# A fifth slot per weight chunk gets half of its remainder by an accumulating transfer, and the first chunk's table load and gate sums are moved forward

## The chip, the cores and the metric

The kernel runs on one core of a Trainium2 chip. The metric is the device time of one execution in microseconds. The core has five engines that run their own instruction streams and meet through semaphores: TensorE (PE in the profile; PEld is its weight load), VectorE (DVE), ScalarE (ACT), GpSimd (POOL) and SyncE (SP). Transfers are issued by SP (all weights), by POOL and, a few, by ACT.

## The reference, cut to what matters

One decoder block on a sequence of 256 rows of width 2048, in float32:

```python
x = x + 0.5 * swiglu(rmsnorm(x, ffn1_norm), ffn1_wg, ffn1_wu, ffn1_wd)
x = x + hybrid_mixer(rmsnorm(x, mix_norm), ...)      # conv group and sparse attention group
x = x + 0.5 * swiglu(rmsnorm(x, ffn2_norm), ffn2_wg, ffn2_wu, ffn2_wd)
return rmsnorm(x, final_norm)

def swiglu(h, wg, wu, wd):                           # D_FF = 5632
    return (jax.nn.silu(h @ wg) * (h @ wu)) @ wd
```

The change touches the two SwiGLU layers only, called FFN 1 and FFN 2 here (`f` is 0 and 1 in the code).

## The kernel before

**Products in pieces.** Every float32 operand is split into a rounded part and a remainder, `hi` and `lo`. A product is three matmuls: `x_hi w_hi`, `x_hi w_lo` and `x_lo w_hi`. The weights `wg` and `wu` (2048 x 5632) are taken in 11 chunks of 512 columns. A chunk has 16 slots; a slot (a "group") is 256 rows of one of the two matrices, 128 partitions x 2 x 512, and a slot of the kind GATE or UP costs TensorE 12 matmuls of 512 columns: two halves `kk` of the slot, two row tiles of 128, three products. Four slot buffers (`SLOTS = 4`) hold `raw`, `w_hi` and `w_lo`, used in turn. Two neighbouring slots of the kinds PAIR and PAIR2 are computed with seven products in place of eight; for them VectorE makes sums `wt` of the raw weights, and ScalarE and VectorE split these into `wt_hi` and `wt_lo`.

**One slot's way.** SP loads `raw` (512 KB) once `w_lo` of the slot four before is made (`load`). ScalarE rounds it (`hi`, L1365) once the load has landed and TensorE is through with the slot four before. VectorE subtracts (`lo`, L1883) to get `w_lo`. TensorE waits for `lo_ready` in `group` and runs the 12 matmuls (L818 to L820). Each of these engines takes the slots strictly in order, with the other work of a chunk at fixed slots in between.

**Moved slots.** In chunks 2 to 10 (`THREE`), slots 0 to 3 (`MOVED_AT`) have the second half of their remainder made another way. `minus` on ScalarE writes the negated rounded weights into `w_lo[:, s, 1, :]` (L1356), and `remainder` on GpSimd issues a transfer of the weights' 256 KB from HBM that is added to what stands there (L735). VectorE's `lo` then makes only the first half. `group` on TensorE has a branch for these slots (L798, L800, L806): the eight matmuls with `w_hi` first, then the two with the first half of `w_lo`, then a wait for `lo_moved`, then the last two. In the code:

```python
for kk in range(GK):
    if kk:
        pe.wait_ge(lo_moved[s], 16 * moves(c))
    for t, bank in enumerate(banks):
        ins = mm(ps[:, bank, :], hi[:, k + kk, t * P:t * P + P], w_lo[:, s, kk, :], start=False, ...)
```

`minus(c)` is called at the head of `hi(c)`; it waits for the slot's load and for TensorE's end of the slot four before. GpSimd's order in a chunk is: the transfers of moved slots 0 to 3, then the 16 small block transfers of the previous chunk's `gu` (`gu_blocks`, L726), then transfers of moved slots from 4 on, of which there are none before.

**From one chunk to the next.** A chunk's gate products stand in PSUM banks 0 and 1. At its end ScalarE copies product 1 of the pairs (`product1_copy`, L1443); VectorE adds it and the others into the two banks (`gate_products`: L2020, L2005, L2007, L2022; then `right_sums`: L2013, L2015); ScalarE applies Silu to each bank (`silu`, L1459), and TensorE can start the next chunk, which writes the same banks, once both Silus are done (`silu_done`). For the chunks in `LATE` (0 and 2 to 10) this falls into the next chunk: on VectorE `gate_products` comes behind slot 0's `lo`, on ScalarE the copy and the first Silu come behind slot 0's `hi`, and the second Silu behind slot 1's `hi`. ScalarE's functions live in tables. Ahead of chunk 0's Silu the Sqrt table is loaded in both FFNs, so the first Silu of each FFN is preceded by an ACT_TABLE_LOAD.

Of the kernel before, what the change touches and what calls it, by code (L numbers as in the profile page):

```python
# [8 lines left out]
ACT = mybir.ActivationFunctionType  # L9
# [44 lines left out]
          (PAIR, 2), (PAIR2, 2), (UP, 4), (UP, 5), (PAIR, 3), (PAIR2, 3), (UP, 6), (UP, 7)]  # L54
THREE = (2, 3, 4, 5, 6, 7, 8, 9, 10)
LATE = (0,) + THREE
MOVED_AT = (0, 1, 2, 3)
H_QUAD = {1: 0, 2: 1, 3: 2}
PAIRS = 2

# [1 line left out]
def chunk_table(n):  # L62

    return FIRST if n == 0 else CHUNK3 if n in THREE else CHUNK


def chunk_pairs(n):

    return [p for p, (kind, _) in enumerate(chunk_table(n)) if kind == PAIR]
# [22 lines left out]
def chunk_slot(n):  # L92

    return CHUNK_SLOTS * n + (len(down_job(0)) if n >= PART0[1] else 0)
# [65 lines left out]
def moved_slots():  # L160

    return [FFN0[f] + chunk_slot(n) + p for f in range(2) for n in THREE for p in MOVED_AT]

# [140 lines left out]
def build_program(nc, a, out):  # L304
# [45 lines left out]
    junk = sb("junk", [P, CH], BF16)  # L350
# [114 lines left out]
    ones = consts[:, C_ONE:C_ONE + 1]  # L465
# [9 lines left out]
    with ctx:  # L475
# [219 lines left out]
        def _(pool):  # L695
# [42 lines left out]
            def ffn(f):  # L738
                for n in range(1, NFC):
                    early = [p for p in MOVED_AT if p < 4] if n in THREE else []  # L740
                    late = [p for p in MOVED_AT if p >= 4] if n in THREE else []
                    for p in early:
# [587 lines left out]
        def _(act):  # L1330
# [105 lines left out]
            def product1_copy(f, key, last, i=None):  # L1436


                job = job_no(f, key)
                act.wait_ge(pair_done, count(pair_no(f, last) + 1, i, PAIRS))  # L1440
                if job:
                    act.wait_ge(prod_used, count(job, i, 1))
                act.activation(z[:, 0, :], ps[:, PROD1, :], ACT.Copy).then_inc(prod1_copied, 1)  # L1443
# [18 lines left out]
            def late_silu(f, n, t):  # L1462

                if t == 0:
                    product1_copy(f, n, FFN0[f] + chunk_slot(n) + chunk_pairs(n)[-1])
                    if n + 1 not in (PART0[1], NFC):
                        minus(FFN0[f] + chunk_slot(n + 1) + 1)
                silu(f, n, tiles=(t,))
# [397 lines left out]
        def _(dve):  # L1866
# [91 lines left out]
            def slot(f, c, kind, i=None):  # L1958

                if kind == PAIR2:  # L1960
                    s = c % SLOTS
                    dve.wait_ge(hi_ready, count(c + 1, i, CHUNK_SLOTS))
                    tt(w_lo[:, s, 1, :], raw[:, s, 1, :], w_hi[:, s, 1, :].bitcast(F32),
                       ALU.subtract).then_inc(lo_ready, 1)
                    wt_low(f, c - 1, 1, i)
                else:
                    lo(c, i, CHUNK_SLOTS)
                    if kind == PAIR:
                        weight_sums(f, c, i)
                        wt_low(f, c, 0, i)  # L1970
# [46 lines left out]
            def gate_products(f, n, i=None):  # L2017

                dve.wait_ge(prod1_copied, count(job_no(f, n) + 1, i, 1))
                tt(ps[:, 0, :], ps[:, 0, :], z[:, 0, :], ALU.add).then_inc(gate_added, 1)  # L2020
                product_sums(f, n, i)
                tt(ps[:, 1, :], ps[:, 1, :], z[:, 1, :], ALU.add).then_inc(gate_added, 1)  # L2022
# [128 lines left out]
            def ffn(f):  # L2151
                c = FFN0[f]
                if f == 0:
                    first_operands()
                    x_operand(0, 0, 1)
                    op = [lambda n=n: x_operand(0, n) for n in range(NDC)]
                    after = {2: [op[1]], 3: [lambda: h_sums(0, 0, 0)], 4: [op[2]], 5: [lambda: h_sums(0, 0, 1)],
                             6: [lambda: hs_low(0, 0)], 7: [op[3]], 14: [lambda: variance(RS_FFN1, DM, NDC)],
                             15: [lambda: inverse_root(RS_FFN1)]}
                else:  # L2160
                    after = {1: [lambda: residual(NDC - 1, FFN0[1], 1, att_scale)],
                             2: [lambda: h_sums(1, 0, 0), lambda: h_sums(1, 0, 1)], 3: [lambda: hs_low(1, 0)],
                             4: [lambda: variance(RS_FFN2, DM, 3 * NDC)],
                             5: [lambda: x_operand(2, NDC - 1)], 7: [lambda: inverse_root(RS_FFN2)]}
                for p, (kind, _) in enumerate(FIRST):
                    if f == 0 and p == 0:
                        continue
                    slot(f, c + p, kind)
                    for g in after.get(p, ()):
                        g()  # L2170

                def chunk(n, i=None):
                    c = FFN0[f] + chunk_slot(n)
                    gu_at = 9 if n in THREE else 12
                    for p, (kind, _) in enumerate(chunk_table(n)):
                        slot(f, c + p, kind, i)
                        if n == PART0[1]:
                            if p in TURN_STEPS:
                                left_residual(f, 0, 1, TURN_STEPS.index(p))
                            if p == 3:  # L2180
                                right_residual(f, 1)
                        else:
                            if n == 1 and p in (7, 8):
                                h_sums(f, 1, p - 7)
                            if n == 1 and p == 9:
                                hs_low(f, 1)
                            if n - 1 in LATE and p == 0:
                                gate_products(f, n - 1)
                            if n - 1 in LATE and p == 1:
                                right_sums(f, n - 1)  # L2190
                            if p == 2:
                                up_products(f, n - 1, i)
                                up(f, n - 1, i)
                            if p == 3:
                                gu_transpose(f, n - 1, i)
                            if p == gu_at:
                                gu_sums(f, n - 1, quad_no(f, n - 1), i)
                            if p == gu_at + 1:
                                gu_operand(f, n - 1, quad_no(f, n - 1), i)
                            if p == (14 if n in THREE else gu_at + 1):  # L2200
                                gs_low(n - 1, quad_no(f, n - 1), i)
                        if p == 14 and n not in LATE:
                            gate_products(f, n, i)
                        if p == 15 and n not in LATE:
                            right_sums(f, n, i)

                def down(part):
                    c = FFN0[f] + down_slot(part)
                    n_last = PART0[part] + PARTN[part] - 1
                    order = down_job(part)  # L2210
                    steps_at = left_steps(part)
                    for g, (h, p, kind, _) in enumerate(order):
                        slot(f, c + g, kind)
                        if n_last in LATE and g == 0:
                            gate_products(f, n_last)
                        if n_last in LATE and g == 1:
                            right_sums(f, n_last)
                        if g == 2:
                            up_products(f, n_last)
                            up(f, n_last)  # L2220
                        if g == 3:
                            gu_transpose(f, n_last)
                        if g == (12 if part == 0 else 10):
                            gu_operand(f, n_last, None)
                        if g in steps_at:
                            for step in steps_at[g]:
                                left_residual(f, part, *step)
                        if part == 0 and g == HALF[0] + 4:
                            right_residual(f, 0)
                        if part == 1:  # L2230
                            if g == HALF[1] + 2:
                                residual(1, FFN0[f] + down_slot(1, 1), 1, half)
                            if f == 0 and g == X0_AT + 4:
                                x_operand(1, 0)
                            if f == 1 and g in (23, 25, 39):
                                final_gains((23, 25, 39).index(g))

                for n in range(1, PARTN[0]):
                    chunk(n)
                down(0)  # L2240
                for n in range(PART0[1], NFC):
                    chunk(n)
                down(1)
# [468 lines left out]
```

## Time and profile before

| | us |
|---|---|
| median of 3 timed runs | 1812.42 (1812.26 to 1814.29) |
| profiled execution | 1810.13 |
| its span (first to last instruction) | 1808.3 |
| TensorE busy | 1796.8 |
| VectorE busy | 1544.5 |
| ScalarE busy | 1066.0 |
| GpSimd busy | 309.3 |

The granted TensorE clock was 0.999 of full speed (2.4 GHz) over the span. Times in the rows of the next section are counted from the start of the span. A row of instructions names line, engine, operation, and what is written and read (`out<-in`); busy time of an engine that others don't wait for costs nothing. A group of matmuls has overlapping durations: a matmul of 512 columns shows as 389 ns, and in an unbroken stretch one starts every 227 ns.

### The profile page before, as it was taken

What the parts mean: (1) busy time and instruction counts of PE and PEld (TensorE: products, weight loads), DVE (VectorE), ACT (ScalarE), POOL (GpSimd) and SP (SyncE); (2) the same over time, 40 slices, a digit from 0 to 9 for tenths busy, and PEclk for the clock granted to TensorE, in tenths of its full rate; (3) what the DMA queues carried; (4) which work ended last, traced back from release to release, by engine and by line L of the source; (5) the groups of instructions that cost most, each with busy time, mean ns of one, the idle gap of its engine ahead of it and who ended that gap; (6) DMA issues with size and microseconds to landing.
All of it is one profiled execution on the core that took longest, in us unless ns stands there. A gap on an engine that the chain in (4) does not pass through costs nothing.

```text
span 1808.3 us, 22130 instructions
## 1 busy us (share of the span) xinstructions
PE 1796.8 (99%) x8116; PEld 1477.5 (82%) x8116; DVE 1544.5 (85%) x1893; ACT 1066.0 (59%) x1418; POOL 309.3 (17%) x514
## 2 busy tenths in 40 slices
PE   9999999999999999999999999999999999999998
PEld 7778888888888888888788888888888888888886
DVE  7989998889999987678567867899999879999987
ACT  6656655455666556556577745566665455666554
POOL 1123221002222100000123300122221001332100
PEclk9999999999999999999999999999999999999999
DMA  7778876678888767766543655678886677888764
GB/s 244 208 225 244 251 235 210 207 217 239 235 234 242 221 196 210 209 210 198 151 132 114 210 175 182 207 229 241 236 243 213 205 222 224 238 241 249 242 205 151
DMA packets 209661, 386.20 MB, mean 214 GB/s; under 512 B 20164, under 2 KB 25008, under 8 KB 209424
## 3 DMA queue, kind: packets, MB, share of 16 engines
q1 hardware_dynamic: 185008, 352.37, 62.4%
q0 software_dynamic: 22016, 30.90, 8.1%
q10 hardware_dynamic: 2528, 1.52, 0.3%
q8 instruction: 64, 1.05, 0.2%
q14 instruction: 45, 0.37, 0.1%
HBM read 368.98 MB, written 4.19 MB: 206 GB/s over the span
## 4 chain that ended last, share of the span: by engine, by line
PE 90%; DVE 6%; DMA 2%; ACT 1%; issue 1%; SPq 0%; ACTq 0%; DVEq 0%
PE ps L818 18%; PE ps L820 18%; PE ps L819 18%; PE ps L836 7%; PE ps L838 7%; PE ps L837 7%; PE ps L806 3%; PE ps L798 3%; PE ps L800 3%; DVE w_lo L1883 2%; PE ps L885 2%; DMA raw<-in_ffn_wg_dram 1%; DVE wt_lo L1955 1%; ACT w_hi L1365 1%; DVE wt L1945 1%
## 5 line engine op out<-in xcount | busy, mean ns | idle before, releaser
L1883 DVE TENSOR_TENSOR w_lo<-raw,w_hi 128x1024 fp32r<-128x1024 f32 (+1 forms) x567 | 647.7, 1160 | 115.6 <-ACT w_hi L1365 112.2
L1365 ACT ACTIVATE w_hi<-raw 128x1024 fp32r<-128x1024 f32 x567 | 590.4, 1054 | 217.5 <-PE ps L820 130.2
L818 PE MATMUL ps<-w_hi,hT_hi 128*128 128x512 f32 x972 | 381.7, 393 | 1.5 <-ACT gu L1459 1.2
L820 PE MATMUL ps<-w_hi,hT_lo 128*128 128x512 f32 x972 | 378.9, 390 | 0.0
L819 PE MATMUL ps<-w_lo,hT_hi 128*128 128x512 f32 x972 | 378.6, 389 | 0.0
L1416 ACT ACTIVATE wt_hi<-wt 128x1024 fp32r<-128x1024 f32 x176 | 185.5, 1054 | 286.5 <-DVE wt L1945 286.5
L726 POOL DMA_DIRECT2D gu_raw<-gu_sq x352 | 188.4, 544 | 363.5 <-DVE gu_sq L2129 353.4
L818 PEld LDWEIGHTS ps<-w_hi,hT_hi 128*128 128x128 f32 x972 | 182.6, 188 | 39.6 <-DVE w_lo L1883 2.2
L1955 DVE TENSOR_TENSOR wt_lo<-wt,wt_hi 128x1024 fp32r<-128x1024 f32 x176 | 214.6, 1219 | 0.0
L820 PEld LDWEIGHTS ps<-w_hi,hT_lo 128*128 128x128 f32 x972 | 182.5, 188 | 38.8
L819 PEld LDWEIGHTS ps<-w_lo,hT_hi 128*128 128x128 f32 x972 | 182.6, 188 | 36.5
L818 PE MATMUL ps<-w_hi,guT_hi 128*128 128x512 f32 x496 | 193.0, 389 | 0.0
L820 PE MATMUL ps<-w_hi,guT_lo 128*128 128x512 f32 x496 | 193.0, 389 | 0.0
L819 PE MATMUL ps<-w_lo,guT_hi 128*128 128x512 f32 x496 | 192.9, 389 | 0.0
L735 POOL DMA_DIRECT2D w_lo<-in_ffn_wg_dram x72 | 62.3, 866 | 648.4 <-ACT w_lo L1356 648.4
L1945 DVE TENSOR_TENSOR wt<-raw 128x1024 f32<-128x1024 f32 x88 | 107.5, 1221 | 23.9 <-PE ps L838 10.6
L798 PE MATMUL ps<-w_hi,hT_hi 128*128 128x512 f32 x288 | 112.1, 389 | 0.0
L800 PE MATMUL ps<-w_hi,hT_lo 128*128 128x512 f32 x288 | 112.1, 389 | 0.0
L819 PEld LDWEIGHTS ps<-w_lo,guT_hi 128*128 128x128 f32 x496 | 93.1, 188 | 19.4
L820 PEld LDWEIGHTS ps<-w_hi,guT_lo 128*128 128x128 f32 x496 | 93.1, 188 | 19.4
L818 PEld LDWEIGHTS ps<-w_hi,guT_hi 128*128 128x128 f32 x496 | 93.1, 188 | 19.2
L765 POOL TENSOR_SCALAR prob<-prob,sums,gate 128x128 f32<-128x128 f32 (+1 forms) x64 | 37.2, 590 | 258.8 <-DVE sums L2391 258.8
(320 smaller groups left out, 2790.1 us busy)
## 6 DMA issues: line engine op xcount, KB each, us to landing
raw<-in_ffn_wu_dram SPq DMA_DIRECT2D x176, 512.0 KB, 5.1
raw<-in_ffn_wd_dram SPq DMA_DIRECT2D x176, 512.0 KB, 4.8
raw<-in_ffn_wg_dram SPq DMA_DIRECT2D x175, 512.0 KB, 4.6
raw<-in_w_in_dram SPq DMA_DIRECT2D x88, 512.0 KB, 3.7
w_lo<-in_ffn_wg_dram POOLq DMA_DIRECT2D x72, 256.0 KB, 6.7
raw<-in_w_out_dram SPq DMA_DIRECT2D x32, 512.0 KB, 4.5
gu_raw<-gu_sq POOLq DMA_DIRECT2D x352, 32.0 KB, 3.6
x_parked<-x SPq DMA_DIRECT2D x8, 256.0 KB, 5.3
```

The source lines that it names most:

```text
L726: pool.dma_start(gu_raw[c_ * SQ:c_ * SQ + SQ, :, a_, :], gu_sq[a_ * SQ:a_ * SQ + SQ, :, c_ * P:c_ * P + P]).then_inc(gu_moved, 16)
L798: mm(ps[:, bank, :], hi[:, k + kk, t * P:t * P + P], w_hi[:, s, kk, :], start=begin, stop=False, skip_group_check=skip)
L800: mm(ps[:, bank, :], lo[:, k + kk, t * P:t * P + P], w_hi[:, s, kk, :], start=False, stop=False, skip_group_check=skip)
L818: mm(o, x_hi, w_hi[:, s, kk, :], start=begin, stop=False, skip_group_check=skip)
L819: mm(o, x_hi, w_lo[:, s, kk, :], start=False, stop=False, skip_group_check=skip)
L820: ins = mm(o, x_lo, w_hi[:, s, kk, :], start=False, stop=last and kk == GK - 1, skip_group_check=skip)
L836: mm(o, x_hi, y_hi, start=start, stop=False, skip_group_check=True)
L837: mm(o, x_hi, y_lo, start=False, stop=False, skip_group_check=True)
L1365: act.activation(w_hi[:, c % SLOTS, :, :], raw[:, c % SLOTS, :, :], ACT.Copy).then_inc(hi_ready, 1)
L1416: act.activation(wt_hi[:, 2 * half:2 * half + 2, :], wt[:, 2 * half:2 * half + 2, :], ACT.Copy).then_inc(t_hi_ready, 1)
L1883: tt(w_lo[:, s, 0:own, :], raw[:, s, 0:own, :], w_hi[:, s, 0:own, :].bitcast(F32), ALU.subtract).then_inc(lo_ready, 1)
L1955: tt(wt_lo[:, sl, :], wt[:, sl, :], wt_hi[:, sl, :].bitcast(F32), ALU.subtract).then_inc(t_lo_ready, 1)
```

## The change

Three edits, which all act in both FFNs:

1. `MOVED_AT` gets slot 14. In chunks 2 to 10 the slot (UP, 6) is then a moved slot too: ScalarE writes the negated half ahead of its `w_hi`, GpSimd issues the accumulating transfer (behind `gu_blocks`), VectorE makes half of `w_lo`, and TensorE runs the other branch of `group`, with its wait.
2. On ScalarE a Silu of one element is put behind `product1_copy` of chunk 0, so that the table load belongs to it and not to the first Silu of `gu`.
3. On VectorE `gate_products` of chunk 0 goes from behind slot 0 of chunk 1 to ahead of it.

```diff
--- before.py
+++ after.py
@@ -54,7 +54,7 @@
           (PAIR, 2), (PAIR2, 2), (UP, 4), (UP, 5), (PAIR, 3), (PAIR2, 3), (UP, 6), (UP, 7)]
 THREE = (2, 3, 4, 5, 6, 7, 8, 9, 10)
 LATE = (0,) + THREE
-MOVED_AT = (0, 1, 2, 3)
+MOVED_AT = (0, 1, 2, 3, 14)
 H_QUAD = {1: 0, 2: 1, 3: 2}
 PAIRS = 2
 
@@ -1463,6 +1463,8 @@
 
                 if t == 0:
                     product1_copy(f, n, FFN0[f] + chunk_slot(n) + chunk_pairs(n)[-1])
+                    if n == 0:
+                        act.activation(junk[:, 0:1], ones, ACT.Silu)
                     if n + 1 not in (PART0[1], NFC):
                         minus(FFN0[f] + chunk_slot(n + 1) + 1)
                 silu(f, n, tiles=(t,))
@@ -2173,6 +2175,8 @@
                     c = FFN0[f] + chunk_slot(n)
                     gu_at = 9 if n in THREE else 12
                     for p, (kind, _) in enumerate(chunk_table(n)):
+                        if n == 1 and p == 0:
+                            gate_products(f, n - 1)
                         slot(f, c + p, kind, i)
                         if n == PART0[1]:
                             if p in TURN_STEPS:
@@ -2184,7 +2188,7 @@
                                 h_sums(f, 1, p - 7)
                             if n == 1 and p == 9:
                                 hs_low(f, 1)
-                            if n - 1 in LATE and p == 0:
+                            if n - 1 in LATE and p == 0 and n > 1:
                                 gate_products(f, n - 1)
                             if n - 1 in LATE and p == 1:
                                 right_sums(f, n - 1)
```

## Rows read from the trace of the kernel before

**Rows 1.** The page, busy us of each engine with share and count

```profile
PE 1796.8 (99%) x8116; PEld 1477.5 (82%) x8116; DVE 1544.5 (85%) x1893; ACT 1066.0 (59%) x1418; POOL 309.3 (17%) x514
```

**Rows 2.** TensorE's waits: waited for, us in total, times, longest

```profile
PE ps L818 <- ACT gu L1459: 1.2, 1, 1.2
PE ps L836 <- DVE wt_lo L1955: 0.7, 2, 0.5
```

**Rows 3.** Timeline, TensorE, chunk 0 to 1 of FFN 1: start us, length us, what

```profile
54.50 0.39 PE L820 MATMUL ps<-w_hi,hT_lo 128*128 128x512 f32 x1
56.06 0.50 PE L818 MATMUL ps<-w_hi,hT_hi 128*128 128x512 f32 x1 [1.18 <-ACT gu L1459]
```

**Rows 4.** Timeline, ScalarE, the same place; in brackets idle time and what ended it

```profile
50.17 0.57 ACT L1443 ACTIVATE z<-ps 128x512 f32<-128x512 f32 x1
52.51 1.28 ACT L1459 ACT_TABLE_LOAD   x1 [1.76 <-DVE ps L2020]
53.80 0.69 ACT L1459 ACTIVATE gu<-ps,rs 128x512 f32<-128x512 f32 x1
54.38 1.05 ACT L1365 ACTIVATE w_hi<-raw 128x1024 fp32r<-128x1024 f32 x1
55.33 0.68 ACT L1459 ACTIVATE gu<-ps,rs 128x512 f32<-128x512 f32 x1
```

**Rows 5.** Timeline, VectorE, the same place

```profile
51.73 0.69 DVE L2020 TENSOR_TENSOR ps<-ps,z 128x512 f32<-128x512 f32 x1
...
53.78 0.70 DVE L2022 TENSOR_TENSOR ps<-ps,z 128x512 f32<-128x512 f32 x1
55.47 1.23 DVE L1883 TENSOR_TENSOR w_lo<-raw,w_hi 128x1024 fp32r<-128x1024 f32 x1 [0.99 <-ACT w_hi L1365]
...
64.00 2.32 DVE L1883 TENSOR_TENSOR w_lo<-raw,w_hi 128x1024 fp32r<-128x1024 f32 x2
```

**Rows 6.** Chain that ended last, first and last of 14 pieces before TensorE

```profile
117.80 1.23 DVE wt L1945
...
124.27 1.15 DVE w_lo L1883
```

**Rows 7.** Groups of instructions, ScalarE: busy us, mean ns, idle us before

```profile
L1411 ACT ACT_TABLE_LOAD x2 | 2.6, 1283 | 0.0
```

**Rows 8.** Groups by shape, VectorE, `w_lo` of whole and of moved slots

```profile
L1883 DVE TENSOR_TENSOR w_lo<-raw,w_hi 128x1024 fp32r<-128x1024 f32 x495 | 599.6, 1228 | 103.0 <-ACT w_hi L1365 100.0
L1883 DVE TENSOR_TENSOR w_lo<-raw,w_hi 128x512 fp32r<-128x512 f32 x72 | 49.3, 687 | 12.6 <-ACT w_hi L1365 12.2
```

**Rows 9.** Timeline, slot 14: `w_hi` and 11th matmul, first and last of 18

```profile
132.42 1.99 ACT L1365 ACTIVATE w_hi<-raw 128x1024 fp32r<-128x1024 f32 x2
138.40 0.39 PE L819 MATMUL ps<-w_lo,hT_hi 128*128 128x512 f32 x1
...
1684.57 1.04 ACT L1365 ACTIVATE w_hi<-raw 128x1024 fp32r<-128x1024 f32 x1
1692.52 0.39 PE L819 MATMUL ps<-w_lo,hT_hi 128*128 128x512 f32 x1
```

**Rows 10.** Timeline, chunk 8 of FFN 1, slot 0: negated copy, transfer's issue

```profile
466.81 0.63 ACT L1356 ACTIVATE w_lo<-raw 128x512 fp32r<-128x512 f32 x1 [0.78 <-DMA raw<-in_ffn_wg_dram]
...
467.74 0.93 POOL L735 DMA_DIRECT2D w_lo<-in_ffn_wg_dram  x1 [17.93 <-ACT w_lo L1356]
```

**Rows 11.** Line L735, its 72 accumulating transfers: who waited (us, times); landing

```profile
PEld ps L806: 0.8, 4
...
DMA to landing us min/median/max: 4.2/6.7/7.8
```

**Rows 12.** Windows around the end of chunk 7, FFN 1; last: clock, DMA share, GB/s

```profile
460.00:465.00 5.00, 5.00 (x24) 4.14 (x23) 4.93 (x7) 3.40 (x5) 0.00 (x0) 1.00 0.50 127
...
470.00:475.00 5.00, 5.00 (x24) 4.14 (x23) 4.62 (x8) 4.46 (x8) 1.68 (x2) 1.00 1.05 320
```

**Rows 13.** DMA issues, one chunk's first accumulating transfer (slowest of 18): KB, landing us

```profile
w_lo<-in_ffn_wg_dram POOLq DMA_DIRECT2D x1, 256.0 KB, 7.2
```

## The prediction

> **What bounds the kernel now.** The page comes first: TensorE is busy for 1796.8 of 1808.3 us [rows 1]. The sum is made against this execution: the program took 1810.13 us, 1.83 us more than its span, and the median of the three timed runs, 1812.42 us, lies 2.29 us above that. I assume both offsets stay, so a change of the span is added to the median.
>
> The second view is what TensorE waited for. It names one wait worth having, 1.2 us for ScalarE's `gu` (the second Silu of a chunk), and 0.7 us for `wt_lo`; the rest is smaller [rows 2]. The reader is to see how little there is to win: TensorE goes from matmul to matmul, one every 0.227 us in a stretch without a wait, and no edit to another engine's work can give more than the few waits listed. A gain beyond 0.2% (3.6 us, about what a measurement of this kernel tells from no change) isn't there to be had; a loss is, because TensorE would wait for anything that comes late, 18 times over.
>
> **Part one: the table load.** TensorE's last matmul of chunk 0 in FFN 1 starts at 54.50 and the next at 56.06 [rows 3]. Undisturbed, that one starts at 54.50 + 0.227 = 54.73, so the stall is 1.33 us. ScalarE's rows show its end: copy of product 1 to 50.74, idle 1.76 us, table load 1.28 us from 52.51, Silu, `w_hi` of chunk 1's slot 1, second Silu to 56.01 [rows 4]. The load waits there because it belongs to the Silu, which waits for VectorE's first add into `ps`; that add starts only at 51.73, after `w_lo` of chunk 1's slot 0 [rows 5].
>
> After the change the load has nothing to wait for: 50.74 to about 52.03, plus about 0.2 us for one element. VectorE turns to the sums when the copy is there, 50.78. From its rows the four adds take 53.78 + 0.70 - 51.73 = 2.75 us, to 53.53. The first Silu runs 52.2 to 52.9, `w_hi` to 53.8, the second Silu to 54.5. The moved `w_lo` comes after the sums, 53.43 to 54.65. TensorE needs both, so it starts at about 54.75 and the stall shrinks by 1.3 us. What is queued behind VectorE's new wait is that `w_lo` and everything after; the load of slot 4's weights on SyncE's queue waits for it too, and leaves near 54.7, some 2.8 us later. What hides that is VectorE's order: slot 4's `w_lo` has its turn only at 64.00 [rows 5], 63.1 in the new order, and with 1.05 us for `w_hi` ahead of it the load would have to take over 7.3 us to be late; if it does, the 0.9 us below shrink by as much.
>
> Of the 1.3 us not all stays. VectorE's next `w_lo` started at 55.47 behind 0.99 us of idle time [rows 5]; in the new order it starts at 54.57, 0.9 us earlier. The chain of waits runs through VectorE alone from 117.80 to 125.42 in chunk 2, and only then passes to TensorE, which it makes wait for `w_lo` [rows 6]. There the two engines meet again, and what is left is what VectorE gained: **0.9 us**. The bounds are 0 (all given back) and 1.4.
>
> In FFN 2 the same place holds no stall: the wait for `gu` is counted once in the whole span [rows 2]. There the moved `w_lo` leaves idle time in front of the sums and goes behind them, where VectorE waited 0.99 us in FFN 1 as well. Gain 0; loss at most 0.2, its 1.2 us less that idle time.
>
> A rule was weighed here. ScalarE's rows show two Sqrt table loads of 1283 ns with 0.0 us of idle time before them [rows 7], so a load follows on what went before. The Trainium skill, "ScalarE: Activation LUTs", section "What ACT_TABLE_LOAD costs", gives the same 1283 ns but adds about 1380 ns of drain to each switch; its load would end near 53.4, the Silus would end near 55.7, and only some 0.3 us would be won. The trace contradicts it, and the sum goes by the rows.
>
> **Part two: the 15th slot.** Nine chunks of each FFN gain one moved slot, 18 in all. For each, VectorE's `w_lo` shrinks from 1228 to 687 ns [rows 8], 18 x 0.54 = 9.7 us of VectorE, none of it on TensorE's clock in most chunks. ScalarE gets a negated copy of 0.63 us [rows 10] ahead of `w_hi`: 18 x 0.63 = 11.3 us on an engine busy for 59% [rows 1]. VectorE's `w_lo` of the slot starts up to 0.6 us later and is 0.54 us shorter, so it is ready when it was. GpSimd gets 18 issues of about 0.93 us [rows 10]; the 16 block transfers of the chunk are through by then. The 18 transfers move 4.7 MB more.
>
> What has to be on the path is the transfer itself. It can't start before the negated copy, and that copy stands on ScalarE where `w_hi` of the slot stands now, behind the pair's two `wt_hi`. TensorE needs the sum at the slot's 11th matmul, 10 x 0.227 = 2.27 us after its first. In chunk 2 of FFN 1 `w_hi` starts at 132.42 and the 11th matmul at 138.40: 5.98 us. In chunk 10 of FFN 2 it is 1684.57 and 1692.52: 7.95 us [rows 9]. Read alike, the 18 budgets are 5.98, 6.51, 7.17, 7.91, 8.46, 6.95, 7.02, 6.46, 7.16 in FFN 1 and 5.99, 6.75, 7.04, 7.91, 8.47, 7.73, 6.07, 6.95, 7.95 in FFN 2.
>
> Against that stands copy, issue and landing. From a copy's start to GpSimd's issue it is 467.74 - 466.81 = 0.93 us [rows 10]. From issue to landing the 72 transfers of this kind took 4.2 to 7.8 us, median 6.7 [rows 11]. Which of these is the new one like? The later three of a chunk stand in each other's way: DMA is 1.05 busy in 470 to 475, and moves 320 GB/s, against 0.50 in 460 to 465 just before the new issue [rows 12]. The first of each chunk (18 of them) took 4.2 to 7.2 us, mean 5.8 [rows 13]. The new one, earlier and alone, is nearest to these.
>
> - At 4.2 us: 5.13 in all, below every budget, cost 0.
> - At 5.8 us: 6.73 in all. Five budgets are short, by 0.75, 0.22, 0.27, 0.74, 0.66: 2.6 us.
> - At the median 6.7 us: 7.63 in all. Twelve are short: 11.5 us.
> - At the longest, 7.8 us, all are short: 28.7 us.
>
> I take **1.2 us**, below the 5.8 line, for two reasons. The stretch ahead of the new issue is the emptiest of a chunk. And VectorE, which paces ScalarE up to this slot, gets 0.54 us back in each chunk, so from the second of these chunks on the negated copy comes earlier; the two chunks 2 have no such help and are the shortest, 0.75 us each at 5.8.
>
> The new transfer also stands before the next chunk's four. TensorE already waits for four of the 72, 0.8 us in all [rows 11]. 256 KB at the 300 GB/s of that stretch is 0.85 us; 4 x 0.85 = 3.4 is the upper bound, 0 the lower (a wait in the 15th slot gives the others time). I take **0.3 us**.
>
> **Sum.** -0.9 + 1.2 + 0.3 = +0.6 us: the span goes to 1808.9, the profiled execution to 1810.7, and the median to **1813.0 us**.
>
> **Rivals.**
> - *The transfer lands late nearly everywhere.* For it: half of the 72 took 6.7 us or more, and the budgets hardly exceed 8. Against it: the empty stretch, and that first ones run at 5.8. It decides from a landing of about 6.1 us, where the shortfalls sum to 4.6 us and, with 0.3 and less 0.9, the result is slower by over 0.2%. At 6.7 it is 11.5 + 0.3 - 0.9: 1823 us; half the shortfall, should VectorE's help count, gives 1817.6. Chance 0.19. The Trainium skill, "SBUF — State Buffer", section "SBUF: two separate sides", warns that VectorE can lock GpSimd out of the port through which it writes a transfer's descriptors, which would push this way; the trace shows one issue of 0.93 us [rows 10] beside a VectorE that is busy for 85% [rows 1], and nothing that tells such a lock from GpSimd's own pace.
> - *No transfer is late.* If it lands in under 5 us, part two costs nothing, the waits for `wt_lo` (0.7 us [rows 2]) may go, and the time is 1812.4 - 0.9 to 1812.4 - 1.8: 1811.1 us. Within 0.2%. Chance 0.25.
> - *VectorE's relief is worth more than the waits show.* Matmuls after a wait start slowly, and the waits of [rows 2] may understate what small lags add up to. TensorE would have to shed 3.6 us; all its idle time is 11.5 us, the start and the end of the program within it [rows 1]. Chance 0.03: 1808.
> - *The forecast*, 1811.8 to 1815: chance 0.53.
>
> **Range and chances.** 1810.8 to 1817.5 us. Below it lies most of the third rival and a little spread of the runs (1812.26 to 1814.29 before), above it half of the first; about 0.2 together. Faster by over 0.2% (below 1808.8): 0.03. Slower (above 1816.0): 0.19. Within: 0.78.
>
> **What would show the steps.** Right: the table load of FFN 1 at about 50.8, right behind the copy; TensorE's gap at 54.5 below 0.2 us; a wait for `w_lo` in chunk 2 no smaller than now. 90 transfers with the new ones at 5 to 6 us; TensorE's waits for `DMA w_lo` at 1 to 2 us in all, in chunks 2 first, and VectorE's busy time down by some 10 us. Wrong: waits for `DMA w_lo` in most chunks, summing to over 4.5 us; or a gap at 54.5 as before, which would mean that the load, or the moved `w_lo`, doesn't run where I put it. What would upset the sum is a landing time off by 0.4 us, since the budgets lie so close to it.

## The result and the profile after

The change makes the kernel slower: a median of 1819.58 us (12 executions, 1814.75 to 1822.27) against 1812.45 us for the kernel before (12 executions in the same session, 1811.34 to 1815.21). The ratio (of the means, here and below) is 1.0035, 95% interval 1.0028 to 1.0043: a small loss, but clear of the noise. The prediction, 1813.0 us in a range of 1810.8 to 1817.5, had the direction, a forecast of 0.6 us more, and missed the size, 7.1 us more, which lies outside its range. Its first rival, "the transfer lands late nearly everywhere", gives the place of the loss; the trace shows it at ten of 18 places.

The page of the kernel after, span and busy time of each engine (compare [rows 1]):

```profile
span 1819.1 us, 22185 instructions
...
PE 1802.8 (99%) x8115; PEld 1477.8 (81%) x8116; DVE 1537.8 (85%) x1893; ACT 1073.0 (59%) x1438; POOL 324.9 (18%) x532
```

ScalarE and GpSimd do more (20 and 18 instructions), VectorE less. TensorE's waits in the kernel after (waited for: us in total, times, longest; compare [rows 2]):

```profile
PE ps L806 <- DMA w_lo<-in_ffn_wu_dram: 4.1, 6, 1.0
...
PE ps L836 <- DVE wt_lo L1957: 0.9, 3, 0.5
PE ps L806 <- DMA w_lo<-in_ffn_wg_dram: 0.8, 2, 0.5
```

Two things stand out. The 1.2 us for `gu` is gone, and a new wait for `w_lo<-in_ffn_wu_dram` has come: slot 14 is of the kind UP, the only moved slot that reads `wu`, so this name is the new transfer and no other. The view lists the larger waits only, and counts each from the end that it gives the matmul before, so each comes out some 0.2 us short. Measured from start to start of the two matmuls around the wait for `lo_moved`, less the 0.227 us of an undisturbed step, slot 14 waits in 10 of 18 chunks, 6.0 us in all, and slots 2 and 3 of the next chunk wait 1.6 us.

The transfers' own rows, in the list of issues of the kernel after (count, KB each, median us from issue to landing):

```profile
w_lo<-in_ffn_wg_dram POOLq DMA_DIRECT2D x72, 256.0 KB, 6.5
...
w_lo<-in_ffn_wu_dram POOLq DMA_DIRECT2D x18, 256.0 KB, 6.0
```

**Slot 14 of chunk 2, step by step.** ScalarE, GpSimd and TensorE in the timeline of the kernel after (compare [rows 9, 10]):

```profile
133.75 0.61 ACT L1356 ACTIVATE w_lo<-raw 128x512 fp32r<-128x512 f32 x1
...
134.66 0.94 POOL L735 DMA_DIRECT2D w_lo<-in_ffn_wu_dram  x1 [18.00 <-ACT w_lo L1356]
...
139.26 0.61 PE L806 MATMUL ps<-w_lo,hT_hi 128*128 128x512 f32 x2
140.53 0.73 PE L806 MATMUL ps<-w_lo,hT_hi 128*128 128x512 f32 x2 [0.65 <-DMA w_lo<-in_ffn_wu_dram]
```

The copy starts at 133.75 and the issue at 134.66, 0.91 us later. The issue sees its data land 5.83 us after that, at 140.49, and TensorE goes on at 140.53. It would have gone on at 139.26 + 2 x 0.227 = 139.71: a budget of 5.96 us (I had read 5.98), where copy, issue and landing took 6.74, and 0.82 us lost.

**The front.** ScalarE at the end of chunk 0 of FFN 1, kernel after (compare [rows 4]):

```profile
52.04 0.58 ACT L1443 ACTIVATE z<-ps 128x512 f32<-128x512 f32 x1
52.63 1.28 ACT L1467 ACT_TABLE_LOAD   x1
53.93 0.21 ACT L1467 ACTIVATE junk<-consts 128x1 bf16<-128x1 f32 x1
54.04 0.68 ACT L1459 ACTIVATE gu<-ps,rs 128x512 f32<-128x512 f32 x1
```

The load stands right behind the copy, and the Silu right behind the one element. TensorE there, kernel after (compare [rows 3]; everything is 1.8 us later here, see below):

```profile
56.35 0.39 PE L820 MATMUL ps<-w_hi,hT_lo 128*128 128x512 f32 x1
56.73 0.47 PE L818 MATMUL ps<-w_hi,hT_hi 128*128 128x512 f32 x1
```

The gap went from 1.33 to 0.38 - 0.23 = 0.15 us.

**Where the 10.8 us of the two spans are.** 1.8 us have nothing to do with the change: they arise before the first product matmul. TensorE's start, kernel before:

```profile
5.01 0.66 PE L912 MATMUL ps<-consts,x 128*128 128x128 f32 x4
...
7.92 0.50 PE L927 MATMUL ps<-w_hi,hT_hi 128*128 128x512 f32 x1
```

and kernel after:

```profile
5.73 1.12 PE L912 MATMUL ps<-consts,x 128*128 128x128 f32 x4
...
9.74 0.50 PE L927 MATMUL ps<-w_hi,hT_hi 128*128 128x512 f32 x1
```

Such starts come and go between profiled executions, without regard to the edit: in this form (product matmul at 9.5 or later) it shows in six profiles of the eleven experiments too, five show the other. So I compare profiles from the end of chunk 0 on. The first matmul of chunk 2, kernel before:

```profile
98.56 0.39 PE L798 MATMUL ps<-w_hi,hT_hi 128*128 128x512 f32 x1
```

and kernel after:

```profile
99.58 0.39 PE L798 MATMUL ps<-w_hi,hT_hi 128*128 128x512 f32 x1
```

It is 1.02 us later, so 0.8 us of the 1.8 have been won back by the front. From there to the end the distance grows to 10.8 us, by 9.8: 6.0 + 1.6 us are the waits measured above. The remaining 2.1 us are mostly their shadow: behind each of these 14 waits the second matmul, too, starts 0.11 us late (0.338 us after the first in place of 0.227), which makes 1.5 us. About 0.6 us is left in gaps that I haven't put down to single waits. The medians differ by 7.1 us; a profile is one execution, and its 10.8 us hold the slow start.

### The profile page after: what moved, and what is told of

The parts are those of the page before. It is cut to its first block, busy times and chain, and to the rows that moved or that the text cites. A ratio compares the mean times of both kernels' runs of the same rounds, so it can differ in the third digit from the quotient of the medians.

```text
span 1819.1 us, 22185 instructions
## 1 busy us (share of the span) xinstructions
PE 1802.8 (99%) x8115; PEld 1477.8 (81%) x8116; DVE 1537.8 (85%) x1893; ACT 1073.0 (59%) x1438; POOL 324.9 (18%) x532
## 4 chain that ended last, share of the span: by engine, by line
PE 69%; DVE 14%; DMA 10%; ACT 3%; issue 3%; POOL 1%; ACTq 0%; DVEq 0%; SPq 0%; POOLq 0%
PE ps L818 15%; PE ps L820 15%; PE ps L819 15%; PE ps L836 5%; PE ps L838 4%; PE ps L837 4%; DVE w_lo L1885 4%; DMA raw<-in_ffn_wg_dram 3%; DMA raw<-in_ffn_wu_dram 3%; DMA w_lo<-in_ffn_wu_dram 2%; PE ps L806 2%; DVE wt L1947 2%; DVE wt_lo L1957 2%; PE ps L798 2%; PE ps L800 2%
## 5 line engine op out<-in xcount | busy, mean ns | idle before, releaser
L1885 DVE TENSOR_TENSOR w_lo<-raw,w_hi 128x1024 fp32r<-128x1024 f32 (+1 forms) x567 | 639.6, 1142 | 129.0 <-ACT w_hi L1365 124.1
L819 PE MATMUL ps<-w_lo,hT_hi 128*128 128x512 f32 x900 | 351.1, 390 | 0.0
L820 PEld LDWEIGHTS ps<-w_hi,hT_lo 128*128 128x128 f32 x900 | 169.0, 188 | 36.1
L818 PEld LDWEIGHTS ps<-w_hi,hT_hi 128*128 128x128 f32 x900 | 169.2, 188 | 35.4 <-DVE w_lo L1885 1.6
L819 PEld LDWEIGHTS ps<-w_lo,hT_hi 128*128 128x128 f32 x900 | 169.1, 188 | 33.7
L735 POOL DMA_DIRECT2D w_lo<-in_ffn_wg_dram x72 | 61.2, 850 | 382.8 <-ACT w_lo L1356 381.9
L806 PE MATMUL ps<-w_lo,hT_hi 128*128 128x512 f32 x360 | 100.4, 394 | 5.4 <-DMA w_lo<-in_ffn_wu_dram 4.1
```

What stands on the lines that cost most here:

```text
L818: mm(o, x_hi, w_hi[:, s, kk, :], start=begin, stop=False, skip_group_check=skip)
L819: mm(o, x_hi, w_lo[:, s, kk, :], start=False, stop=False, skip_group_check=skip)
L820: ins = mm(o, x_lo, w_hi[:, s, kk, :], start=False, stop=last and kk == GK - 1, skip_group_check=skip)
L1885: tt(w_lo[:, s, 0:own, :], raw[:, s, 0:own, :], w_hi[:, s, 0:own, :].bitcast(F32), ALU.subtract).then_inc(lo_ready, 1)
```

## The experiments

Each kernel was timed beside the kernel before; all ratios are to it, with 95% intervals. "Waits" are measured from start to start as above, and landings, where a mean is given, are worked out from the 18 transfers of that slot. Where a diff is against the kernel after, it says so.

**One part alone.** Edits 2 and 3 without slot 14 (e1; against after: `MOVED_AT = (0, 1, 2, 3)`).

> Edits 2 and 3 alone (table load and gate sums of the first chunk moved forward; slots 0 to 3 moved as before). Theory A (the loss is the fifth slot's, the front edits win what was forecast): 0.8 to 0.9 us below the kernel before, about 1811.6 us, TensorE's gap between chunk 0 and 1 of FFN 1 at about 0.15 us. Rival B (the front edits cost something later on, for instance through the later load of chunk 1's slot 4): 1 us or more above the kernel before.

Measured: 1810.90 us, ratio 0.9996 [0.9988, 1.0005]. From the end of chunk 0 to the end of chunk 1 the profile is 0.84 us shorter than before's. Then slot 14 without edits 2 and 3 (e2; diff against before):

```diff
-MOVED_AT = (0, 1, 2, 3)
+MOVED_AT = (0, 1, 2, 3, 14)
```

> Edit 1 alone (slot 14 moved, the front as before). Theory A: 7 us above the kernel before, some 1819.5 us, with waits of TensorE for the 15th slot's transfer of 6 us and of 1 to 2 us for slots 2 and 3. Rival B (the front edits share in the loss): within 4 us of the kernel before.

Measured: 1817.99 us, ratio 1.0034 [1.0022, 1.0046]; 6.6 us of waits in slot 14 at a mean landing of 6.15 us, and 0.1 us in slots 0 to 3. Its waits on TensorE:

```profile
PE ps L806 <- DMA w_lo<-in_ffn_wu_dram: 5.1, 8, 1.3
...
PE ps L818 <- ACT gu L1459: 1.2, 1, 1.2
```

The whole loss is slot 14's; the front, about 0.8 us, lies below what these timings tell from nothing. And this profile, which began as the one of before did (chunk 0 ends within 0.05 us of it), ends 7.9 us later: 6.7 us of waits and 11 times the 0.11 us behind a wait.

**The transfer or its surroundings?** (e3) The kernel after with all that slot 14 got but the transfer: VectorE makes the whole remainder over the negated copy, so the same sum is computed, and TensorE keeps the order of matmuls of a moved slot (diff against after; `KEPT` are the 18 slots).

```diff
-    return sum(1 for m in MOVED if m <= c and m % SLOTS == c % SLOTS)
+    return sum(1 for m in MOVED if m not in KEPT and m <= c and m % SLOTS == c % SLOTS)
...
-                    late = [p for p in MOVED_AT if p >= 4] if n in THREE else []
+                    late = []
...
-                own = 1 if c in MOVED else GK
+                own = 1 if c in MOVED and c not in KEPT else GK
```

> The changed kernel, but slot 14's transfer isn't issued and VectorE makes the whole remainder; ScalarE's negated copy and TensorE's other order of matmuls stay. Theory A (the lateness of the transfer is the cost): the loss is gone, 0 to 1 us below the kernel before, 1811.5 to 1812.5. Rival C (ScalarE's extra 0.63 us ahead of w_hi, or TensorE's other branch, is the cost): still 5 us or more above the kernel before.

Measured: 1811.78 us, ratio 0.9998 [0.9989, 1.0007]. ScalarE's copy and the other order of matmuls cost nothing that can be seen; the transfer and VectorE's shorter share make the 0.37% between this kernel and the one after.

**Another slot.** (e4, against after.)

```diff
-MOVED_AT = (0, 1, 2, 3, 14)
+MOVED_AT = (0, 1, 2, 3, 15)
```

> The changed kernel with slot 15 moved in place of slot 14. In the trace before, w_hi of slot 15 starts at 464.98 in chunk 7 and the 11th matmul of that slot comes at 473.7: a budget of 8.7 us where slot 14 had 6.95. Copy, issue and landing took 6.5 to 8.9 us for slot 14. Theory A (a budget too short by some tenths): waits for this slot's transfer fall from 6.0 to below 1 us and the time to about 1812 to 1813.5, the rest being the next chunk's slots. Rival D (the extra 4.7 MB in a crowded stretch is the cost, whichever slot it belongs to): 1817 us or more.

Measured: 1820.24 us, ratio 1.0051 [1.0035, 1.0068]. Slot 15 itself waits 0.4 us in all, with budgets of 7.7 to 9.5 us and a mean landing of 6.7 us. But the waits have moved, as TensorE's list shows:

```profile
PE ps L806 <- DMA w_lo<-in_ffn_wg_dram: 3.6, 6, 1.1
...
PE ps L806 <- DMA w_lo<-in_ffn_wu_dram: 0.2, 1, 0.2
```

Slots 0 to 3 of the next chunk wait 0.2, 2.7, 0.6 and 1.8 us, and land on average after 7.25 us in slot 0 and 7.03 in slot 1, against 6.44 and 5.91 in the kernel after. The budget is longer by 1 us or more, and the kernel is no faster: the waits are at the next transfers, which this one stands before.

**The same transfer, asked for earlier.** (e5) ScalarE makes the negated half ahead of slot 13's work in place of behind it (against after):

```diff
                     for p, (kind, _) in enumerate(chunk_table(n)):
+                        if p == 13:
+                            minus(c + 14)
                         slot(f, c + p, kind, i)
```

> The changed kernel with slot 14's negated copy made ahead of slot 13's w_hi on ScalarE, some 1.5 us earlier (in the trace before that place is 462.56 in chunk 7, against 464.03). Theory A (slot 14's budgets are some tenths short of 7.1 us for copy, issue and landing): waits for slot 14 fall from 6.0 to below 0.7 us. If the waits are all there is to it, the time is 1811 to 1813. Theory D, added since the run with slot 15 (a transfer also pushes its neighbours in the queue): the earlier one is further from the next chunk's, whose waits stay at 0 to 2 us. Rival C (ScalarE's extra work ahead of the pair's second half is the cost): waits for wt_lo of over 3 us appear instead, and the time stays above 1817.

Measured: 1812.45 us beside 1811.88 before, ratio 1.0004 [0.9995, 1.0014]. ScalarE and GpSimd in chunk 2:

```profile
131.18 0.62 ACT L1356 ACTIVATE w_lo<-raw 128x512 fp32r<-128x512 f32 x1
131.70 0.61 ACT L1424 ACTIVATE w_hi<-raw 128x512 fp32r<-128x512 f32 x1
132.22 1.04 ACT L1416 ACTIVATE wt_hi<-wt 128x1024 fp32r<-128x1024 f32 x1
133.16 2.00 ACT L1365 ACTIVATE w_hi<-raw 128x1024 fp32r<-128x1024 f32 x2
...
132.09 0.94 POOL L735 DMA_DIRECT2D w_lo<-in_ffn_wu_dram  x1 [15.76 <-ACT w_lo L1356]
```

The copy stands ahead of 1.5 us of other ScalarE work (131.70 to 133.16) in place of behind it. The budgets become 7.4 to 9.5 us, 8.7 on average, the 18 transfers land after 5.8 us on average, and slot 14 waits nowhere. It is the same transfer, as large, in the same chunk; only its start is earlier, and the loss of 0.35% is gone.

**The same transfer, asked for later.** (e6) The copy goes behind `w_hi` of the slot, and the load that reuses the buffer waits for it as well (against after):

```diff
+                if c - SLOTS in LATE_COPY:
+                    sp.wait_ge(minus_ready, MOVED.index(c - SLOTS) + 1)
...
-                minus(c)
+                late = c in LATE_COPY
+                if not late:
+                    minus(c)
...
+                if late:
+                    minus(c)
```

> The changed kernel with slot 14's negated copy behind the slot's w_hi instead of ahead of it, about 1 us later; all work is the same (SyncE's load of the slot four further on waits for the copy as well). Theory A: every budget is 0.95 to 1.05 us shorter; with a landing of 6.2 us the shortfalls add up to 17 to 19 us, and the time is near 1829. Theory D alone (what counts is the amount moved, not when it starts): under 1822.

Measured: 1840.53 us, ratio 1.0158 [1.0144, 1.0172]; 22.4 us of waits in slot 14, mean landing 7.09 us. TensorE's list, in which one name now holds nearly all:

```profile
PE ps L809 <- DMA w_lo<-in_ffn_wu_dram: 19.9, 15, 3.3
```

With the early copy this is a scale of three marks for one and the same transfer: ahead of 1.5 us of ScalarE's work, no waits; as changed, 6.0 us; behind `w_hi`, 22.4 us. Why it was more than expected: copy to use, without the stall, measures 6.80 us on average against 7.11, and the landing is 7.09 against 6.21, so of the 1.2 us that each slot is worse off, 0.3 are the lost budget and 0.9 a slower landing, which I had not foreseen. What made it slower isn't shown: the edit also holds back the load that reuses the buffer. The median is 28.7 us above before's, more than the waits; the last section shows what follows on a long one.

**Do the neighbours hold it up?** (e7) Slot 0 is no longer a moved slot, so that a chunk has four transfers as before (against after):

```diff
-MOVED_AT = (0, 1, 2, 3, 14)
+MOVED_AT = (1, 2, 3, 14)
```

> The changed kernel without slot 0 in the list: slots 1, 2, 3 and 14 are moved, so there is as much transferred as before the change and nothing follows slot 14's transfer for about 5 us. Theory A (the landing of slot 14's own transfer is too long for its budget, whoever follows): slot 14's landing stays near 6.1 us and its waits at 4 to 6 us, time 1815 to 1818. Theory D (the neighbours make it slow): its landing falls to 5.3 us or less and its waits below 1.5 us, time 1811 to 1813.

Measured: 1814.60 us beside 1811.88 before, ratio 1.0011 [1.0002, 1.0020]. Slots 1 to 3 no longer wait at all, slot 14 still does:

```profile
PE ps L806 <- DMA w_lo<-in_ffn_wu_dram: 2.8, 5, 0.7
```

Its waits are 4.1 us from start to start at a mean landing of 6.06 us, against 6.21 in the kernel after. So slot 14's landing isn't the work of the transfer that follows it. What a fifth transfer costs the following ones is less certain. They wait nowhere here and 1.6 us in the kernel after; but slots 0 to 3 also wait 0.75 us in e1 and 0.7 us in e3, where there is no fifth transfer, and only 0.1 us in e2, where there is one.

**Half the bytes.** (e9) Slot 14's transfer moves 128 KB, VectorE makes the other columns (against after, the core; `width` is used in the negated copy too):

```diff
+                width = CH // 2 if c in HALVED else CH
+                pool.dma_start(w_lo[:, s, 1, 0:width], w[:, GK * q + 1, n * CH:n * CH + width],
                                accum_op=ALU.add).then_inc(lo_moved[s], 16)
...
+                if c in HALVED:
+                    cols = slice(CH // 2, CH)
+                    tt(w_lo[:, s, 1, cols], raw[:, s, 1, cols], w_hi[:, s, 1, cols].bitcast(F32), ALU.subtract)
```

> The changed kernel with half of slot 14's transfer: 256 of its 512 columns (128 KB) come by the accumulating transfer and ScalarE's negated copy is as much shorter, VectorE makes the other 256. Theory A: copy, issue and landing get shorter by 0.3 us for the copy and by whatever of the landing's 6.2 us goes with its size; with a landing near 5.2 us the waits fall below 0.5 us and the time to 1811 to 1812.5. Rival E (the landing is mostly a fixed time or time spent behind the raw loads issued before it): landing 5.8 us or more, waits above 2 us, time 1814 or more.

Measured: 1813.88 us beside 1812.07 before, ratio 1.0008 [0.9999, 1.0017]. The list of issues has:

```profile
w_lo<-in_ffn_wu_dram POOLq DMA_DIRECT2D x18, 128.0 KB, 5.3
```

Half the bytes land on average after 5.4 us in place of 6.2, only 0.8 us sooner; the shorter copy gives another 0.2 us. Slot 14's waits fall to 0.4 us, slots 1 to 3 keep 1.4 us, about what the time lies above the 1812.5 us that I had expected at most. Most of a landing isn't bytes.

**The front's two edits one by one.** Edit 2 alone (e8, against before: the one-element Silu only), and edit 3 alone (e10, against before: `gate_products` ahead of slot 0 only).

> Edit 2 alone: the one-element Silu that carries the table load, with VectorE's order as before. From the rows of the kernel before the first Silu starts at about 52.5 instead of 53.80, slot 1's w_hi ends at 54.2, the second Silu waits for the second bank's sum (54.48) and ends at 55.2: TensorE's gap is 0.5 to 0.6 us instead of 1.33. If what is won in the end is VectorE's earlier w_lo of slot 1 (55.47, now 54.4), TensorE is 0.8 to 1.0 us ahead at the end of chunk 1, as with both edits. If edit 3 is what wins, 0.3 us or less is left there.

> Edit 3 alone: VectorE's sums of chunk 0 ahead of its w_lo, the table load where it was. From the rows of the kernel before the load waits for the first sum (51.5), ends at 52.8, the Silus at 53.5 and 55.2: TensorE's gap 0.5 to 0.6 us, as with edit 2 alone, and 0.8 to 0.9 us won at the end of chunk 1. If the forecast's reason (VectorE's earlier w_lo of slot 1) is right, edits 2 and 3 are alternatives, not terms of a sum: both together won 0.84, edit 2 alone 0.92.

Measured: edit 2 alone 1810.34 us beside 1811.88 before, ratio 0.9993 [0.9984, 1.0002]; edit 3 alone 1811.13 us beside 1812.07, ratio 0.9997 [0.9988, 1.0006]. The times tell neither from nothing; the profiles do. From the end of chunk 0 to the end of chunk 1, edit 2 saves 0.92 us, edit 3 saves 0.82, and both together 0.84. TensorE's place with edit 2 alone:

```profile
54.55 0.39 PE L820 MATMUL ps<-w_hi,hT_lo 128*128 128x512 f32 x1
55.36 0.50 PE L818 MATMUL ps<-w_hi,hT_hi 128*128 128x512 f32 x1 [0.42 <-ACT gu L1459]
```

The gap is still 0.58 us, more than with both, and yet nothing is lost by the end of chunk 1: there VectorE's lead decides and not the gap, as the prediction had it. The kernel after shows where the difference goes. With both edits TensorE comes 0.42 us (start to start) too early for VectorE's next `wt_lo`:

```profile
85.14 0.50 PE L836 MATMUL ps<-wt_hi,hs_hi 128*128 128x512 f32 x1 [0.26 <-DVE wt_lo L1957]
```

With edit 2 alone there is no wait at this place. The two edits are alternatives.

**What the experiments point to.** (e11) Edit 2 alone, slots 1, 2, 3 and 14, and the early copy (diff against before):

```diff
-MOVED_AT = (0, 1, 2, 3)
+MOVED_AT = (1, 2, 3, 14)
...
                     product1_copy(f, n, FFN0[f] + chunk_slot(n) + chunk_pairs(n)[-1])
+                    if n == 0:
+                        act.activation(junk[:, 0:1], ones, ACT.Silu)
...
+                        if p == 13:
+                            minus(c + 14)
                         slot(f, c + p, kind, i)
```

> A version put together from the runs so far: edit 2 alone at the front, slots 1, 2, 3 and 14 moved (as many as before the change), slot 14's negated copy ahead of slot 13's w_hi. With an early copy slot 14 should have no wait, and with slot 0 out of the list slots 1 to 3 none either (in the run with slots 1, 2, 3 and 14 they had 0.0 us). Theory A: 0.8 to 1.8 us below the kernel before, and no better than edit 2 alone, since TensorE has nothing else to shed: 1810 to 1811. If it is slower than the kernel before, something other than the transfers' lateness comes with slot 14.

Measured: 1809.17 us beside 1812.07 before, ratio 0.9984 [0.9975, 0.9993]: 0.16% faster than the kernel before, with the same number of transfers, and clearly faster than the kernel after. What the moved slots add to edit 2 isn't shown: edit 2 alone had 0.9993 [0.9984, 1.0002], and the intervals overlap. No wait for a transfer is left in any of the 72 places. The largest wait on TensorE outside the start is

```profile
PE ps L818 <- ACT gu L1459: 1.2, 3, 0.4
```

## Why the prediction was wrong

**Right: the front.** Load behind the copy, the gap below 0.2 us (0.15), 0.9 us left of it by chunk 2 where VectorE paces (0.83 in the kernel after, 0.92 with edit 2 alone). What I missed is that either edit alone gives the whole. The load in its new place starts right behind the copy and the next operation right behind the load, so the drain of 1380 ns that the Trainium skill, "ScalarE: Activation LUTs", section "What ACT_TABLE_LOAD costs", adds to a switch isn't to be seen after the change either.

**Right: the mechanism and its arithmetic.** Budgets by slot 14's copy and 11th matmul, less copy, issue and landing, were the right account. The 18 unstalled budgets measured after have a mean of 7.11 us (mine had 7.14), copy to issue 0.91 us (I had 0.93). The prediction named a landing of 6.1 us as the point from which the result is slower by over 0.2%. It is 6.21 us (5.63 to 7.99), and put into my own table of budgets, with 0.91 for copy to issue, this gives 5.5 us; 6.0 us were measured. What the sum had no term for is the 0.11 us behind each wait, 1.5 us in all. e5 and e6 show the same balance from both sides.

**The step that failed** is the value that the prediction took out of this arithmetic: "I take **1.2 us**, below the 5.8 line, for two reasons." Measured: 6.0 us. Both reasons fell.

- *"The stretch ahead of the new issue is the emptiest of a chunk."* True, and beside the point: a transfer lives in the stretch behind its issue. The stretch behind it, which I had not read, in the kernel before, and under it chunk 2's two in the kernel after (columns as in [rows 12]: TensorE, its loads, VectorE, ScalarE, GpSimd, then granted clock, DMA share, GB/s):

```profile
465.00:470.00 5.00, 5.00 (x24) 4.14 (x23) 4.82 (x6) 3.63 (x6) 0.93 (x1) 1.00 0.82 243
```

```profile
130.00:135.00 5.00, 4.97 (x23) 3.79 (x22) 4.93 (x7) 3.69 (x5) 0.34 (x1) 1.00 0.57 144
135.00:140.00 5.00, 4.88 (x22) 3.71 (x20) 4.83 (x7) 3.33 (x5) 1.46 (x2) 1.00 0.92 238
```

  In 460 to 465 DMA is 0.50 busy, as [rows 12] had it; in 465 to 470 it is already 0.82, before there is any new transfer. The new one meets the next chunk's weight loads: in 135 to 140 DMA is 0.92 busy. It behaves like the 72 (median 6.5 in the same trace), only a little faster, and not like the quickest. That the busy stretch makes the landing long is not shown, though. The DMA share of the 5 us behind the issue, as a mean over the 18 chunks, is 0.90 for slot 14 in the kernel after, 0.83 in e6 and 0.96 for slot 1 in e7, and the landings are 6.21, 7.09 and 4.58 us: the share doesn't sort them. What sets a landing stays open; what is shown is that neither the empty stretch ahead nor being the first of its kind gave one below 5.6 us in the kernel after.
- *"VectorE ... gets 0.54 us back in each chunk."* VectorE's half is shorter, 688 in place of 1228 ns, as this group of the kernel after shows:

```profile
L1885 DVE TENSOR_TENSOR w_lo<-raw,w_hi 128x1024 fp32r<-128x1024 f32 x477 | 578.0, 1228 | 103.0 <-ACT w_hi L1365 99.4
...
L1885 DVE TENSOR_TENSOR w_lo<-raw,w_hi 128x512 fp32r<-128x512 f32 x90 | 61.8, 688 | 26.0 <-ACT w_hi L1365 24.7
```

  The copy does not come earlier for it, counted to TensorE's use: the budgets have the same mean. If one chunk gains anything, it is gone by slot 14 of the next.

**The neighbours' term**, 0.3 us, was also too small: slots 2 and 3 wait 1.6 us in the kernel after. It varies by profile (0.1 us in e2, 0.5 in e5, 1.4 in e9, and 0.75 and 0.7 in e1 and e3 without a fifth transfer), so a value between the two bounds, 0 and 3.4, is what can be held. The 0.8 us in four places that it started from was misread: [rows 11] give the idle time of the weight load (PEld), and start to start no matmul behind a wait for `lo_moved` is late in the kernel before. e4 shows where the term becomes the larger one: some 5.2 us when the new transfer is one slot later.

**The rival** that came true was priced at 1817.6 us with half of VectorE's help and 1823 without. 0.19 was too low a chance for a mechanism whose decision point, 6.1 us, lay between the two values that the traces offered, 5.8 and 6.7. That 1817.6 lies near the measured 1819.6 is in part luck: it takes a landing of 6.7 us, where 6.2 was measured, and halves the waits for a help of VectorE's that did not come; the two errors offset each other.

**Still open.** What sets a landing, from which the whole loss follows; and the 0.6 us of the profile that no single wait accounts for. The medians' 7.1 us and the 10.8 us of the two profiles agree: before's profiled execution lies 2.3 us below its median, after's 1.3 us above.

## What to carry to other kernels

When work is handed to a transfer, write its budget (from the instruction that frees its start to the first use) beside copy, issue and landing, and take the landing from the bulk of the transfers of its kind, not from the quickest, since neither the stretch ahead of the issue nor the one behind it told the landing here. Where the mean need equals the mean budget (7.12 and 7.11 us here), expect a loss at about half the places (10 of 18), and treat a mean that hides them with suspicion. The remedy is to start it earlier, with work of the issuing chain that doesn't need to come first, before making it smaller or moving it: moving the copy past 1.5 us of other work gave back all of the 0.35% here, and another slot lost no less. Two edits that remove the same stall are worth one of them.

## What the runs showed of the hardware

**A long wait costs TensorE more than its length.** TensorE in chunk 2 of the kernel with the late copy:

```profile
138.05 0.61 PE L809 MATMUL ps<-w_lo,hT_hi 128*128 128x512 f32 x2
141.92 0.87 PE L809 MATMUL ps<-w_lo,hT_hi 128*128 128x512 f32 x2 [3.25 <-DMA w_lo<-in_ffn_wu_dram]
142.59 0.63 PE L821 MATMUL ps<-w_hi,hT_hi 128*128 128x512 f32 x1
143.01 0.63 PE L822 MATMUL ps<-w_lo,hT_hi 128*128 128x512 f32 x1
```

and the windows around it (the clock is the column of 1.00 and 0.57):

```profile
138.00:142.00 4.00, 0.74 (x4) 0.28 (x3) 3.86 (x7) 2.84 (x4) 0.84 (x1) 1.00 1.01 230
142.00:146.00 4.00, 4.00 (x11) 3.14 (x12) 0.91 (x2) 1.58 (x2) 0.83 (x1) 0.57 1.09 304
146.00:150.00 4.00, 4.00 (x19) 3.28 (x18) 2.94 (x4) 1.77 (x3) 0.84 (x1) 1.00 1.07 323
```

Behind the wait matmuls start 0.42 to 0.43 us apart in place of 0.227, and the granted clock of the stretch is 0.57, for the most part the level of 1.2 GHz in place of 2.4. It lasted for about eight matmuls, some 1.6 us in all, and came after the waits of 3.42, 2.72 and 2.11 us in this profile; behind none of up to 1.8 us did it show. From the first matmul of chunk 2 to the end this profile is 28.5 us longer than before's. The waits are 22.8 us (0.4 of them slot 3's), the three slow stretches 4.8, the 0.11 us behind each of 17 waits 1.9: 29.5 us in all, 1 us more than the difference, so the account is close and not exact.

**A short wait costs more than its length, too.** Behind each of the 14 waits of the kernel after, from 0.19 to 1.19 us long, the second matmul started 0.338 us after the first in place of 0.227; in the rows of slot 14 of chunk 2 above, two matmuls take 0.73 us behind the wait and 0.61 ahead of it. The granted clock was full there.

**Landing is mostly not bytes.** 256 KB land after 6.2 us and 128 KB after 5.4 us at the same place; if each further 128 KB takes the same 0.8 us, some 4.6 of the 6.2 us go with no byte (an estimate from these two). The place counts as well: in e7 slot 1's transfer, issued while no other of its kind is under way, took 4.6 us on average, and slot 0's in the kernel before, also alone at its issue, 5.8.

**The start of the program varies by 1.8 us** between profiles, and the clock goes with it. Six matmuls ahead of the first product, kernel before:

```profile
6.41 1.46 PE L943 MATMUL ps<-junk 128*128 128x512 bf16 x6
```

and kernel after:

```profile
7.49 2.19 PE L943 MATMUL ps<-junk 128*128 128x512 bf16 x6
```

In the kernel before they start 0.216 us apart, in the kernel after the first ones 0.427 us, the pace of the slow stretches above. The views print a granted clock of 1.00 for both, but the trace has no record of it ahead of 4.47 us in the kernel before and of 8.96 in the kernel after, where its record of the full clock begins. In the six quick starts of the 13 profiles this record begins at 4.0 to 5.3 us, in the seven slow ones at 8.9 to 10.4. So a late full clock goes with the slow start, without exception; what delays it was not tried.
